# A two-block network on one core: the first norm taken token group by token group, and two clears moved behind it

## The reference, cut to what matters

```python
def _layer_norm(x, g, b):
    xf = x.astype(jnp.float32)
    mu = jnp.mean(xf, axis=-1, keepdims=True)
    var = jnp.mean(jnp.square(xf - mu), axis=-1, keepdims=True)
    y = (xf - mu) * lax.rsqrt(var + LN_EPS)
    return (y * g.astype(jnp.float32) + b.astype(jnp.float32)).astype(x.dtype)
```

## Time and profile before

| | us |
|---|---|
| median of 3 runs | 765.91 (765.05 to 765.91) |
| span of the profiled execution | 764.1 |
| TensorE busy in it | 746.7 (98%) |
| VectorE / ScalarE / GpSimd busy | 574.5 / 465.9 / 143.2 |
| share of the chain that ended last: TensorE / VectorE / ScalarE | 84% / 7% / 5% |

### The profile page before, as it was taken

The page is one execution under the profiler, slowest core; times in us unless marked ns, Lnnn a source line. Parts: engine busy times, 40 slices in busy tenths (PEclk is TensorE's granted clock), DMA queues, the critical chain, the costliest instruction groups (busy, mean ns, idle before and its releaser), DMA issues.

```text
span 764.1 us, 14615 instructions
## 1 busy us (share of the span) xinstructions
PE 746.7 (98%) x5421; PEld 681.4 (89%) x5421; DVE 574.5 (75%) x853; ACT 465.9 (61%) x783; POOL 143.2 (19%) x143
## 2 busy tenths in 40 slices
PE   8999999999999999999999999999999999999996
PEld 7999999888999889898889888997888999999994
DVE  7897989843877477777584668888787898866675
ACT  6767775567674475554544537668686555555554
POOL 5000000001125023333232220010003211343331
PEclk9999999999999999999999999999999999999999
DMA  8455443144445789798788880853236665555541
GB/s 297 126 182 165 138 134 116 56 139 166 143 162 196 258 241 328 248 315 296 244 270 282 279 313 32 316 212 106 84 111 220 228 242 192 189 189 195 177 134 55
DMA packets 46295, 148.54 MB, mean 194 GB/s; under 512 B 9356, under 2 KB 10252, under 8 KB 46240
## 3 DMA queue, kind: packets, MB, share of 16 engines
q1 hardware_dynamic: 44688, 144.88, 56.2%
q10 hardware_dynamic: 1552, 2.91, 1.3%
HBM read 145.64 MB, written 1.05 MB: 192 GB/s over the span
## 4 chain that ended last, share of the span: by engine, by line
PE 84%; DVE 7%; ACT 5%; issue 2%; POOL 1%; DMA 1%; SPq 0%; DVEq 0%; ACTq 0%; POOLq 0%
PE ps L799 30%; PE ps L742 21%; PE ps L494 17%; PE ps L508 3%; PE ps L524 2%; DVE wl L1677 1%; ACT wh L1116 1%; PE ps L594 1%; PE ps L613 1%; PE ps L756 1%; PE ps L1035 1%; PE ps L977 1%; ACT prob L1485 1%; PE ps L543 1%; DMA raw<-in_w_stream 1%
## 5 line engine op out<-in xcount | busy, mean ns | idle before, releaser
L1677 DVE TENSOR_TENSOR wl<-raw,wh 128x1024 fp32r<-128x1024 f32 x220 | 282.4, 1287 | 108.1 <-ACT wh L1116 107.0
L1116 ACT ACTIVATE wh<-raw 128x1024 fp32r<-128x1024 f32 x220 | 231.5, 1054 | 67.9 <-PE ps L742 48.7
L799 PE MATMUL ps<-xh,wh 128*128 128x256 f32 x672 | 190.0, 283 | 0.4 <-issue 0.3
L799 PE MATMUL ps<-xh,wl 128*128 128x256 f32 x672 | 188.5, 280 | 0.0
L799 PE MATMUL ps<-xl,wh 128*128 128x256 f32 x672 | 188.4, 280 | 0.0
L799 PEld LDWEIGHTS ps<-xh,wh 128*128 128x128 f32 x672 | 126.7, 188 | 5.0 <-issue 2.6
L799 PEld LDWEIGHTS ps<-xl,wh 128*128 128x128 f32 x672 | 126.6, 188 | 1.9
L799 PEld LDWEIGHTS ps<-xh,wl 128*128 128x128 f32 x672 | 126.8, 189 | 0.0
L494 PE MATMUL ps<-xh,wh 128*128 128x256 f32 (+1 forms) x400 | 117.1, 293 | 0.8 <-DVE wl L1677 0.6
L494 PE MATMUL ps<-xh,wl 128*128 128x256 f32 (+1 forms) x400 | 113.6, 284 | 0.0
L494 PE MATMUL ps<-xl,wh 128*128 128x256 f32 (+1 forms) x400 | 113.3, 283 | 0.0
(11 more groups left out here) (412 smaller groups left out, 1244.2 us busy)
## 6 DMA issues: line engine op xcount, KB each, us to landing
raw<-in_w_stream SPq DMA_DIRECT2D x220, 512.0 KB, 3.7
ada_w<-in_w_ada SPq DMA_DIRECT2D x48, 512.0 KB, 5.5
vtk<-in_x SPq DMA_DIRECT2D x2, 512.0 KB, 4.6
out<-ob SPq DMA_DIRECT2D x4, 256.0 KB, 2.1
u<-uT SPq DMA_DIRECT2D x16, 34.0 KB, 2.5
eepp<-in_s_mats SPq DMA_DIRECT2D x1, 512.0 KB
bti<-btr SPq DMA_DIRECT2D x16, 32.0 KB, 2.4
ws<-in_w_s ACTq DMA_DIRECT2D x1, 512.0 KB, 6.4
```

Source lines behind the costliest of these rows:

```text
L799: mm = nc.tensor.matmul(ps[:, bank, 0:SEQ], w, x, start=(k == 0), stop=(k == 3 * KD - 1))
L1116: nc.scalar.activation(wh[:, b % RING], raw[:, b % RING], ACT.Identity).then_inc(hi_done, 1)
L1677: V.tensor_tensor(wl[:, b % RING], raw[:, b % RING], wh[:, b % RING].bitcast(F32), ALU.subtract).then_inc(lo_done, 1)
```

## The change

The norm is taken group by group: each token tile gets its own root (with epsilon added as the root's bias), its own reciprocal and its own scaling. ScalarE scales the meta tile and x, VectorE scales x2. TensorE turns k = 0 to 5 of the meta tile, then of x, then of x2, with calls of `keep_running` between (18, 6, 10 and 3, instead of 15, 3, 4, 3 and 7); k = 6 and 7 are turned as before. GpSimd's clears of `cpi` and `toep` go behind its wait for the eighth turn.

```diff
@@ -315,7 +315,7 @@
-        LN_BASE = {"var": (0, 1, 3), "std": (0, 1, 3, 3, 5, 7), "rstd": (0, 0, 2, 2, 4, 6), "norm": (0, 3, 4, 4, 5),
+        LN_BASE = {"var": (0, 3, 5), "std": (0, 3, 5, 5, 7, 9), "rstd": (0, 2, 4, 4, 6, 8), "norm": (0, 2, 3, 3, 4),
                    "norm_act": (0, 0, 3, 3, 6), "turned": (0, 8, 16, 16, 24), "h": (0, 8, 16, 16, 24), "hi": (0, 8, 16, 16, 24),
                    "lo": (0, 8, 16, 16, 24)}
         LN = {what: sem(f"ln_{what}") for what in LN_BASE}
@@ -525,26 +525,33 @@
             zeros = std[:, 0:P]
             pe.wait_ge(S["cleared"], 1)
-            keep_running(15, 0, zeros)
-            pe.wait_ge(S["x2_landed"], 16)
+            keep_running(18, 0, zeros)
+            pe.wait_ge(S["ident_landed"], 16)
+            pe.wait_ge(LN["norm"], 1)
+            def turn_x(k, n):
+                a, z = J[n]
+                return nc.tensor.transpose(ps[:, LN0_BANK[k], a:z], xt[n][0:z - a, k * P:(k + 1) * P], ident[0:z - a, 0:z - a])
+            for k in range(6):
+                turn_x(k, 0)
+            pe.wait_ge(LN["var"], 2)
+            keep_running(6, 0, zeros)
+            pe.wait_ge(LN["rstd"], 2)
+            keep_running(10, 0, zeros)
+            pe.wait_ge(LN["norm"], 2)
+            for k in range(6):
+                turn_x(k, 1)
             keep_running(3, 0, zeros)
-            pe.wait_ge(S["ident_landed"], 16)
-            keep_running(4, 0, zeros)
-            pe.wait_ge(LN["var"], 1)
-            keep_running(3, 0, zeros)
-            pe.wait_ge(S["x2_scale"], 1)
-            keep_running(7, 0, zeros)
-            pe.wait_ge(LN["norm"], 3)
-            def turn_x(k):
-                if k >= 6:
-                    pe.wait_ge(LN["h"], k - 5)
-                for n, (a, z) in enumerate(J):
-                    mm = nc.tensor.transpose(ps[:, LN0_BANK[k], a:z], xt[n][0:z - a, k * P:(k + 1) * P], ident[0:z - a, 0:z - a])
+            pe.wait_ge(S["x2_scaled"], 1)
+            for k in range(6):
+                turn_x(k, 2).then_inc(LN["turned"], 1)
+            for k in range(6, KD):
+                pe.wait_ge(LN["h"], k - 5)
+                for n in range(3):
+                    mm = turn_x(k, n)
                 mm.then_inc(LN["turned"], 1)
-            for k in range(KD):
-                turn_x(k)
             first_blocks(B_U, (0, 1), lambda k: (LN["lo"], k + 1), 0)
             for b in range(B_U + 2, B_V):
                 stream(b, 0)
@@ -1118,10 +1125,14 @@
             half_pi = hb[:, 51:52]
             act.wait_ge(S["lam_landed"], 16)
             nc.scalar.activation(dt, span("log_dt"), ACT.Exp).then_inc(S["half_done"], 1)
-            act.wait_ge(LN["var"], 1)
-            nc.scalar.activation(lnr[:, :, 0], lnr[:, :, 1], ACT.Sqrt).then_inc(LN["std"], 1)
-            act.wait_ge(S["x2_scale"], 1)
-            nc.scalar.activation(xt[2], xt[2], ACT.Identity, bias=lnr[:, 2, 1:2], scale=lnr[:, 2, 0:1]).then_inc(LN["norm"], 1)
+            for n in range(3):
+                r = META if n == 0 else P
+                act.wait_ge(LN["var"], n + 1)
+                nc.scalar.activation(lnr[0:r, n, 0:1], lnmv[0:r, n, 1:2], ACT.Sqrt, bias=eps[0:r, 1:2]).then_inc(LN["std"], 1)
+                if n < 2:
+                    act.wait_ge(LN["rstd"], n + 1)
+                    nc.scalar.activation(xt[n][0:r, :], xt[n][0:r, :], ACT.Identity, bias=lnr[0:r, n, 1:2], scale=lnr[0:r, n, 0:1])\
+                        .then_inc(LN["norm"], 1)
             hi(0)
             hi(1)
             act.wait_ge(S["cols_landed"], 16)
@@ -1682,27 +1693,44 @@
             V.memset(eps[:, 2:3], RMS_EPS)
             V.memset(lam[:, 0, 0, :], 1.0)
             V.memset(lam[:, 1, 0, :], 0.0)
-            step(V.memset(lnr[:, :, :], 1.0))
-            for n, name in enumerate(("meta_landed", "x_landed", "x2_landed")):
+            def token_stats(n, q):
                 r = META if n == 0 else P
-                dve.wait_ge(S[name], 16)
-                for q in range(2):
-                    V.bn_stats(lnst[0:r, n, q, :], xt[n][0:r, q * 512:(q + 1) * 512]).then_inc(dve_step, 1)
-                step.n += 2
+                V.bn_stats(lnst[0:r, n, q, :], xt[n][0:r, q * 512:(q + 1) * 512]).then_inc(dve_step, 1)
+                step.n += 1
+            def token_moments(n):
+                r = META if n == 0 else P
                 dve.wait_ge(dve_step, step.n)
-                step(V.bn_aggr(lnmv[0:r, n, :], lnst[0:r, n, :, :].rearrange("p a b -> p (a b)")))
-                ins = V.tensor_scalar(lnr[0:r, n, 1:2], lnmv[0:r, n, 1:2], LN_EPS, None, ALU.add)
-            ins.then_inc(LN["var"], 1)
-            dve.wait_ge(LN["std"], 1)
-            step(V.reciprocal(lnr[:, :, 0], lnr[:, :, 0]))
-            V.scalar_tensor_tensor(lnr[:, 2, 1:2], lnmv[:, 2, 0:1], -1.0, lnr[:, 2, 0:1], ALU.mult, ALU.mult).then_inc(S["x2_scale"], 1)
-            for n in (1, 0):
+                V.bn_aggr(lnmv[0:r, n, :], lnst[0:r, n, :, :].rearrange("p a b -> p (a b)")).then_inc(LN["var"], 1)
+            def token_factor(n):
                 r = META if n == 0 else P
-                V.tensor_scalar(xt[n][0:r, :], xt[n][0:r, :], lnmv[0:r, n, 0:1], lnr[0:r, n, 0:1], ALU.subtract, ALU.mult)\
-                    .then_inc(LN["norm"], 1)
+                dve.wait_ge(LN["std"], n + 1)
+                step(V.reciprocal(lnr[0:r, n, 0:1], lnr[0:r, n, 0:1]))
+                if n < 2:
+                    V.scalar_tensor_tensor(lnr[0:r, n, 1:2], lnmv[0:r, n, 0:1], -1.0, lnr[0:r, n, 0:1], ALU.mult, ALU.mult)\
+                        .then_inc(LN["rstd"], 1)
+            dve.wait_ge(S["meta_landed"], 16)
+            token_stats(0, 0)
+            token_stats(0, 1)
+            token_moments(0)
+            token_factor(0)
+            dve.wait_ge(S["x_landed"], 16)
+            token_stats(1, 0)
+            token_stats(1, 1)
+            token_moments(1)
+            dve.wait_ge(S["x2_landed"], 16)
+            token_stats(2, 0)
+            token_factor(1)
+            token_stats(2, 1)
+            token_moments(2)
+            token_factor(2)
+            V.tensor_scalar(xt[2], xt[2], lnmv[:, 2, 0:1], lnr[:, 2, 0:1], ALU.subtract, ALU.mult).then_inc(S["x2_scaled"], 1)
             def split(tag, src, first):
@@ -2400,8 +2428,6 @@
             G.memset(std[:, 0:P], 0.0).then_inc(S["cleared"], 1)
             G.memset(bti[:, :, :], 0.0).then_inc(S["cleared"], 1)
             G.memset(cpr, 0.0).then_inc(S["c_cleared"], 1)
-            G.memset(cpi[:, :, :, :], 0.0).then_inc(S["c_cleared"], 1)
-            G.memset(toep, 0.0).then_inc(S["c_cleared"], 1)
             def hm_lo(m):
                 pool.wait_ge(S["hm_f"], m + 1)
@@ -2409,6 +2435,8 @@
                     .then_inc(S["hm_lo"], 1)
             pool.wait_ge(LN["turned"], KD)
+            G.memset(cpi[:, :, :, :], 0.0).then_inc(S["c_cleared"], 1)
+            G.memset(toep, 0.0).then_inc(S["c_cleared"], 1)
             G.memset(vtk[:, :, :, DV:DV + 1], 1.0).then_inc(pool_step, 1)
             for c in range(CH):
                 pool.wait_ge(S["y_hi"], c + 1)
```

More of the change, by code:

```diff
@@ L296, in two_blocks @@
         S = {n: sem(n) for n in (
-            "x_landed", "x2_landed", "meta_landed", "lam_landed", "cols_landed", "ident_landed", "consts_landed", "x2_scale", "gates_landed",
+            "x_landed", "x2_landed", "meta_landed", "lam_landed", "cols_landed", "ident_landed", "consts_landed", "x2_scaled", "gates_landed",
             "stored",
```

## The result

| | before | changed |
|---|---|---|
| median | 765.56 us (6 runs, 765.05 to 766.23) | 768.47 us (6 runs, 766.97 to 770.97) |
| ratio, 95% interval | | 1.0039 (1.0028 to 1.0049) |
| profiled execution: device time / span / mean granted clock | - / 764.1 / 0.999 | 769.57 / 767.6 / 0.994 |

The change makes the kernel slower by 2.9 us. Not all of that lies in the span (from the first to the last instruction): the six executions have 1.8 to 2.7 us around their spans, where the profiled one of before had 1.8, and the median of their spans is 765.95 us (765.2 to 768.3). So the two medians of the changed kernel lie 2.5 us apart, and some 0.7 of the 2.9 us stand outside what a trace can show.

What follows compares the result with a forecast made beforehand. The prediction took the chain of waits, TensorE alone at the start, as the bound. It summed +0.35 us for TensorE and +2.9 for the clears, taken as +3.3, to 769.2 us against 765.9, range 766.0 to 770.9.

Steps and rivals of the forecast that it cites:

- TensorE's part, +0.35: Filler, turns and passages before the first block matmul: net +0.35 us, between -0.2 and +0.85.
- Casts held by clears: In the first split, the moved clears hold VectorE's casts of tile 3 and the next: +2.9 us by the first blocks' end.
- The argument from two rows: A 1024-column scaling took 1855 ns beside a clear, 789 without; at 285.77 us a scaling and GpSimd instructions waited in turn.
- The rule beside it: GpSimd and two-port VectorE instructions exclude each other; two-input ones contend only with GpSimd reads: +3.2 us, or +3.9 if subtractions were held.
- Onward: After the first blocks: `lo` at 28.70 us is +3.2 us late through ScalarE, which stays to 41.6 us; cleared buffers cost nothing.
- The clock: Rival: TensorE's clock falls while it waits for `xl[2]` and `xl[3]`, 2.3 us more, 771.5 us; chance 0.04.
- stayed for 4.6 us, as at the start: If TensorE's clock fell in the first blocks, it would stay at the lower level for 4.6 us, losing 2.3 us.
- The sum, +3.3 us in the span: Whole kernel: +0.35 and +2.9 us, some tenths more if clears follow without a gap; span 764.1 becomes 767.4 us.
- what the start loses reaches the end one for one: Whole chain of waits: a gain or loss at the start reaches the end in full if it reaches the first blocks' end.
- clears hold no cast: Rival, first split: casts run freely beside the clears, leaving only +0.35 us (-0.2 to +0.85), 766.3 us; chance 0.17.
- x2's turns begin when scaled: Rival, norm: x2's turns do not wait for the filler, -2.6 us, 763.3 us if no cast is held; chance 0.07.
- comes out even: With x2's turns starting early and clears from 12.3 to 16.4 us holding casts, the kernel would neither gain nor lose.

## Why the prediction was right

Predicted 769.2 us (766.0 to 770.9), slower with 0.75; measured 768.47 us, ratio 1.0039. By its own steps:

- **TensorE's part, +0.35.** The x2 turns were put at 14.85, the evacuations at 15.2, the first block matmul at 16.8 us; they came at 15.03, 15.43 and 16.92: +0.5 us against 16.41. The terms hold (three sets of turns on the chain 0.47, 0.66 and the last; filler at the same pace). What was off is the first filler, 6.84 us for 36 records instead of 6.3 (2.79 to 9.1), because its pace doubled later in that execution, at 8.2 instead of 7.4 us. (The prediction calls the two paces two levels of the clock. The pace fits them; but the granted clock of the profile reads 1.00 through all of both fillers, so it does not confirm it.) The moment is not a constant: the same 36 records took 5.81 to 7.17 us in the traces of the changed norm, with no edit that touches them.
- **Casts held by clears.** Tile 3's cast held until the first clear ends (19.3 predicted, 19.5 seen), `xl[2]` at 19.9 (19.96), the waiting cast getting in between the clears, clear 2 to 21.3 (21.37), `xl[3]` at 21.85 (21.86), TensorE at tile 3 at 21.9 (21.92). The argument from two rows, a scaling held by a clear and an alternation between GpSimd and VectorE, carried over to an instruction a quarter as long. The weakest link, that a cast is of the scaling's kind, was shown by the held casts themselves, and by the casts with two inputs, which were not held.
- **The rule beside it** (Trainium skill, SBUF — State Buffer, section "Who interferes with whom"): that an instruction with two SBUF inputs is not shut out by a GpSimd instruction that only writes, as a clear does. The trace of before could not show it; the subtraction of 0.42 us at 19.54 and the 2.36 us for two of 1024 columns do.
- **Onward.** "+3.2 us stays" to 41.6 us: the part that is not the clock did, and VectorE's idle time before its `lo` shrank from 2.25 to 1.48 us, as its slack says. The clears' users did not wait.
- **The clock** was a rival with 0.04 and a price of 2.3 us. In both profiled executions of the change it fell, for 3.4 us, at 1.6 us. The steps that failed are the bound "stayed for 4.6 us, as at the start", and the chance, which leaned on one wait of 1.2 us with no fall: here two waits, 1.3 and 0.9 us, came with 1 us of work between them. It is not in every execution: 3.4 us at half speed alone make the mean clock 0.998, and the fastest one (766.97 us) has 0.999.
- **The sum, +3.3 us in the span.** Seen +3.5 in this pair of executions, but the agreement is partly luck: 3.2 + 1.6 at the start, minus 0.45 between executions, minus 0.72 from the two pauses in the second half, which nothing in the prediction had. The median agrees by luck too: it holds 0.7 us that lie outside the span, which the prediction put at 1.8 us for both kernels, and taken again the changed kernel came to 770.17 us. What holds is the direction and the mechanism, with 3.2 us at tile 3 as worked out. It said that what the start loses reaches the end one for one; by these rows it does, up to such pauses.
- **The rival "clears hold no cast"** (766.3 us) is what the experiment with the clears at the start gives (765.7), and fell by the timelines. **"x2's turns begin when scaled"** fell as argued: TensorE worked through all 37 calls. Its figure, 763.3 us, is close to what the kernels without those calls reached (762.2 to 762.8), if the clears are moved too; its remark that with the clears it "comes out even" was too kind by 2 us (767.7), since it left out the clock's fall, 2.4 us in that trace.

## What to carry to other kernels

What a GpSimd memset costs need not stand in its own row but can stand in VectorE's: before moving one, list which VectorE casts and `tensor_scalar` scalings (even of 16 columns) run beside its new place and who waits for them; put it beside subtractions with two inputs, `bn_stats`, or idle VectorE. If a row of the cover is long (filler of fixed length), look for the second wait behind it before you cut it: here the gain of a shorter filler showed only once the clears were out of the way, 3 us with both. Price a wait of TensorE with what the clock does behind it: with short filler and late clears that was 2.4 us, more than the 0.7 us by which the second tile was late. Compare at least two executions of each kernel before you explain half a microsecond, and line up the same instruction in several kernels to tell scatter from a step that belongs to the code.

## What the runs showed of the hardware that was not expected

- A `tensor_scalar` of 128x16 elements waits for a clear as a large one does (1.40 instead of 0.18 us), while one of 128x1 (0.15 us) and a `bn_stats` of 128x512 (0.68 us) do not. The clear that follows a held instruction is longer: the second of two clears took 1.96 or 1.97 us where a cast waited, 1.80 or 1.81 where none did.
- The clock fell after two waits of 1.3 and 0.9 us, 1 us apart, in both traces of the change, inside a wait of 3.2 us in the short filler with late clears, there for 6.8 us, and at 174.3 us, 2 us behind a wait of 2.3 us, with the clears one place later. It did not after one wait of 1.2 us in the trace of before, nor after one of 0.9 us where the clears were moved alone. In the shorter filler of the kernel before it was at its lower level from 14.9 to 18.3 us; the only wait of any length ahead of it was one of 0.32 us that ended at 11.9 us, and 3 us of turns stood between. What brought it down there is not shown:

```profile
14.90:18.30 3.40, 3.40 (x15) 2.69 (x14) 3.40 (x13) 2.99 (x6) 0.12 (x1) 0.50 0.78 273
```

- The two pauses of 0.4 us, in code that the change does not touch, stand in all four traces with the old norm and in none of the eight with the new one. Why is open.
